# Attention transposes of the mixing stage move from the middle of a gate projection to the seam between two projections, one unit later

## The chip, the cores and the metric

The kernel runs on one core of one Trainium2 chip. The metric is the device time of one execution in microseconds (us), as the median of several runs. The engines are TensorE (PE for its matmuls, PEld for its weight loads), VectorE (DVE), ScalarE (ACT), GpSimd (POOL) and SyncE (SP), which starts the transfers. They run side by side and wait for each other on semaphores. Matmuls write to PSUM, which has eight banks of 512 fp32 columns for each partition.

## The reference, cut to what matters

A transformer block (feed-forward, token mixing, feed-forward) is followed by two layers of another kind. 256 tokens of width 2048 go through all of them. The change touches the token mixing alone:

```python
proj = h @ w_in                       # queries, keys, values of three mixers; then 3 x 2048 gate columns
o_a = _dilated_mixer(...)             # 12 heads in three groups, 4 outputs
o_b = _sink_swa_mixer(...)            # 8 heads, banded, with sinks
o_c = _nsa_mixer(...)                 # 12 heads; compressed, selected and windowed keys
gates = sigmoid(br_gate)
merged = gates[0] * (o_a @ w_branch_a) + gates[1] * (o_b @ w_branch_b) + gates[2] * (o_c @ w_branch_c)
return merged @ w_out
```

Each mixer computes softmax(q k + bias) v for each head.

## The kernel before

**Weights.** Every weight matrix comes as a numbered sequence of slabs (128 x 1024 fp32). SP loads a slab into a ring of four staging buffers. ACT rounds it to its high part (L1538, counted by `hi_done`). POOL (L852) or DVE (L2041) computes the low part, which is the difference. Here the split slabs lie in a ring of three. PE multiplies both parts: 16 matmuls with the high part (L900) and 8 with the low part (L906). A matmul and its weight load make a pair. Four slabs of 24 matmuls make one *product*, which is 256 output columns of a projection for all 256 tokens. It accumulates in one PSUM bank. Banks 0 and 2 alternate from product to product.

**Gates and attention side by side.** The gate columns are 24 products, steps 0 to 23. The attention is cut into 24 *units*: units 0 to 3 for the first mixer (kind a), 4 to 11 for the second (kind b), 12 to 23 for the third (kind c). A unit is a pair of heads and one half of the tokens: T=1 (the later half, which sees two blocks of keys) for even units and T=0 for odd ones. On PE a unit has three parts:

- *scores* (`scores_of`, L1246): q times k into banks 4 to 6. The contraction has 64 rows, so the trace names their tile 64\*128.
- *transposes* (`transposes_of`, recorded at L890 in its helper): the probabilities, block by block, into banks 1, 7 and 5. Their tile is 128\*128, as that of a product. There are 12 or 6 for kind a, 4 or 2 for kind b, 10 or 6 for kind c.
- *V products* (`values_of`, L1265): into 64 rows of bank 3, tile 128\*64. Kind c has four more with 15 rows of contraction. PE records two matmuls for each score and for each V product.

Between them DVE adds the bias and takes the maximum (`bias_of`), ACT takes the exponential (`exps`, L1729), DVE divides (`normalise`), and ACT copies the transposed blocks from PSUM to SBUF (`pt_copies`, L1740 and L1743). After the V products DVE copies the output out (`head_out`, L2323). Probabilities and their transposed copies have two buffers, one for each T.

**The order is written out by hand** for each engine. PE at step s runs the scores of unit s, two slabs of product s, the transposes of unit s-1, the other two slabs, and the V products of unit s-1. ACT copies the blocks of unit s-1 at the end of its step s, and DVE runs `head_out` of unit s-2 in step s. After step 23 come the branch matmuls. For them the output of every fourth unit is rounded and split (`heads_hi`, `heads_rest`). The transposes of unit 23 follow the first slab of the first branch, its V products the second slab. In `transposes_of` PE waits for the probabilities and for the copies of the unit before; in `values_of` for the unit's copies and the output copy of the unit before; in `scores_of` for the bias of the unit before.

Of the kernel before, what the change touches and what calls it, by code (L numbers as in the profile page):

```python
# [25 lines left out]
P = 128  # L26
S = 256
# [14 lines left out]
NCMP, CMP_STRIDE, CMP_END = 15, 16, 31  # L42
# [69 lines left out]
VALUES = {7: (0, 2), 8: (2, 2), 9: (4, 2), 12: (6, 1), 16: (7, 1), 17: (8, 1)}  # L112
CMP_GROUP = 0
LAST_OF = ((0, 6, 9), (4, 12, 12), (12, 17, 17))
HEADS_AT = {6: 0, 10: 1, 14: 2, 18: 3, 22: 4}
A_COLS, B_Q, C_Q, C_KV = 2304, 2304, 3072, 3840
CGATE0, GATE0 = 4608, 4644
# [7 lines left out]
SL_A, SL_B, SL_C = slopes(12), slopes(8), slopes(12)  # L125
# [158 lines left out]
def build(nc, a, out, const, marks, final):  # L284

    ctx = ExitStack()
    with ctx:
# [353 lines left out]
        def units_mix():  # L641
# [31 lines left out]
            for j in range(6):  # L673
                for T in (1, 0):
                    n = (T + 1) * P
                    w = 2 * n + NCMP
                    q, cd = qk[:, 17 + j, :], cst("cdist")[:, T * NCMP:(T + 1) * NCMP]
                    big = {(g, i): segment(4 + 2 * g, i * n, g * w + i * n, n, q, qk[:, 23 + i, :], g, T, dist_of(4, T), SL_C[j + 6 * g])
                           for g in range(2) for i in range(2)}
                    small = [segment(5 if T else 4 + 2 * g, g * S if T else 2 * n, g * w + 2 * n, NCMP, q, kc[:, :], g, T, cd, SL_C[j + 6 * g])  # L680
                             for g in range(2)]
                    segs = [small[0], big[1, 0], big[0, 0], big[1, 1], big[0, 1], small[1]]
                    blks = [block_of(g, g * w + i * n + kb * P, P, vn[:, kb, 7 + i, g * DH:(g + 1) * DH])
                            for i in range(2) for kb in range(T + 1) for g in range(2)]
                    blks += [block_of(g, g * w + 2 * n, NCMP, vc[0:NCMP, g, :]) for g in range(2)]
                    unit(T, w, segs, blks, 6 + j, kind="c", gate=j,
                         softmax=[(g * w + at, m) for g in range(2) for at, m in ((2 * n, NCMP), (0, n), (n, n))])
# [197 lines left out]
        def _(pe):  # L885
# [432 lines left out]
            def product_midway(step):  # L1318

                if step > 0:  # L1320
                    if step == 1:
                        pe.wait_ge(*act_out.after("gn"))
                    transposes_of(first[step - 1])
                else:
                    pe.wait_ge(*act_out.after("pln", PROJ - 1))
                    scores_of(first[0])

            for step in range(len(first)):
                for unit, normed, values in LAST_OF:
                    if step == unit:  # L1330
                        pe.wait_ge(*vec_out.after("qk", normed))
                        pe.wait_ge(*act_out.after("vn", values))
                if step == 12:
                    pe.wait_ge(*vec_out.after("kc"))
                if step > 0:
                    scores_of(first[step])
                product(gg + 1 + step, sA + 4 * step, midway=step)
                if step == 0:
                    pe.wait_ge(evacuated, gg + 1)
                    pe.wait_ge(*act_out.after("vn", PROJ - 1))  # L1340
                    for T in range(TT):
                        last = transpose(ps[:, 7, T * 36:T * 36 + 36], u(CTMP, 36, S)[:, T * P:(T + 1) * P])
                    last.then_inc(*pe_out.mark("gn"))
                else:
                    values_of(first[step - 1])


            def heads(c):
# [4 lines left out]
            for _k in range(4):  # L1353
                for half in range(2):
                    pe.wait_ge(evacuated, g - 1)
                    last = split_passes(acc(g), n, heads(0), True, True, chunks=2, width=512, col0=half * W2)
                    last.then_inc(*((slab_done, 1) if half == 1 else part_done.mark(g)))
                    g += 1
                n += 1
                if _k == 0:  # L1360
                    transposes_of(first[-1])
                if _k == 1:
                    values_of(first[-1])
# [153 lines left out]
        def _(act):  # L1517
# [234 lines left out]
            for step in range(len(first) + 1):  # L1752
                n = sA + 4 * step
                round_upto(n + 2)
                if step == 1:
                    act.wait_ge(*pe_out.after("gn"))
                    for T in range(TT):
                        last = fn(gn[:, T, :], ps[:, 7, 36 * T:36 * T + 36], ACT.Tanh, scale=half_rstd[:, T:T + 1])
                    last.then_inc(*act_out.mark("gn"))
                if step > 0:  # L1760
                    p = step - 1
                    act.wait_ge(evacuated, gg + 1 + p + 1)
                    fn(merged[:, 2 * p:2 * p + 2, :], merged[:, 2 * p:2 * p + 2, :], ACT.Tanh, scale=0.5).then_inc(*act_out.mark("gate", p))
                if step < len(first):
                    round_upto(n + (3 if step else 5))
                    exps(first[step])
                    round_upto(n + 4)
                if step > 0:
                    pt_copies(first[step - 1])
                if step in HEADS_AT:  # L1770
                    heads_hi(HEADS_AT[step], step - 3)
            n = sA + 4 * GATES
            round_upto(n + 6)
            heads_hi(5, -1)
            n += 12
# [121 lines left out]
        def _(dve):  # L1897
# [435 lines left out]
            for step in range(len(first) + 1):  # L2333
                if step > 0:
                    p = step - 1
                    dve.wait_ge(slab_done, sA + 4 * step)
                    v.tensor_tensor(merged[:, 2 * p:2 * p + 2, :], acc(gg + 1 + p).rearrange("p (c s) -> p c s", c=2), by_token(2), ALU.mult
                                    ).then_inc(evacuated, 1)
                if step < len(first):
                    slab_lo(sA + 4 * step + 2)  # L2340
                    bias_of(first[step])
                if step > 1:
                    head_out(first[step - 2])
                if step - 1 in HEADS_AT:
                    heads_rest(HEADS_AT[step - 1])
                if step == 2:
                    dve.wait_ge(*act_out.after("gn"))
                    chained(v.tensor_scalar(gn[:, :, :], gn[:, :, :], 0.5, 0.5, ALU.mult, ALU.add), "gn")
                if step < len(first):
                    normalise(first[step])  # L2350
# [18 lines left out]
            for pair in range(8):  # L2369
                dve.wait_ge(*((slab_done, n + pair // 2 + 1) if pair % 2 else part_done.after(g)))  # L2370
                merge(0, pair, g)
                g += 1
                if pair == 5:
                    head_out(first[-1])
            n += 4
# [389 lines left out]
```

## Time and profile before

| | |
|---|---|
| median of 3 runs | 3058.35 us (3056.56 to 3059.95) |
| the profiled execution | 3059.76 us |
| its span, first to last instruction | 3057.9 us |
| mean granted clock of TensorE | 0.999 |
| PE matmuls | 18842, busy 3038.1 us (99% of the span) |
| DVE, ACT, POOL busy | 66%, 48%, 43% |
| the 24 steps of gates and attention | about 970 to 1299 us of the span |

The profiled execution is 1.4 us above the median of the runs. The table is read from the span and the busy shares: how often an engine works says only whether it can be the bound. Where PE is busy without a gap, its time is the time from the start of one group of matmuls to the start of the next. A row of the timeline gives the start of a group and the time to the end of its last matmul. Matmuls overlap, and their ends are modelled, so what a group costs PE is the difference of two starts.

### The profile page before, as it was taken

The numbers are of one execution on the slowest core, as the hardware profiler recorded it, in microseconds if no ns is written. First come the engines' busy times: TensorE is split into PE (matmuls) and PEld (weight loads), VectorE is DVE, ScalarE is ACT, GpSimd is POOL, SyncE is SP. The second block draws the span as 40 slices with busy tenths as digits, with TensorE's granted clock in tenths as the row PEclk, the third lists the DMA queues.
The fourth block names the chain that finished last, engine by engine and source line by source line (L and its number), as shares of the span: only waits on it lengthen the run. The fifth ranks groups of instructions, "written<-read, shape, count | busy, mean of one in ns | idle before, by whom it ended". The sixth has DMA issues, their size and how long they took to land.

```text
span 3057.9 us, 46756 instructions
## 1 busy us (share of the span) xinstructions
PE 3038.1 (99%) x18842; PEld 2691.0 (88%) x18842; DVE 2009.3 (66%) x2972; ACT 1462.8 (48%) x1922; POOL 1305.8 (43%) x646
## 2 busy tenths in 40 slices
PE   8999999999999999999999999999999999999998
PEld 7888888888999999998888888888999998999987
DVE  4777666664324446787566666577579867689764
ACT  5444444444667445544544444444544454534454
POOL 5455545445556555595544455444340004610013
PEclk9999999999999999999999999999999999999999
DMA  6877787885776554465688887787576445655455
GB/s 218 287 269 260 273 282 246 289 285 183 225 170 177 157 161 145 150 174 200 216 272 279 269 271 263 261 287 268 180 207 191 156 141 197 182 185 177 155 163 179
DMA packets 486896, 661.17 MB, mean 216 GB/s; under 512 B 70024, under 2 KB 273528, under 8 KB 486424
## 3 DMA queue, kind: packets, MB, share of 16 engines
q1 hardware_dynamic: 481192, 653.74, 65.9%
q0 software_dynamic: 4448, 2.94, 0.3%
q8 instruction: 148, 2.42, 0.3%
q10 hardware_dynamic: 1040, 1.52, 0.1%
q14 instruction: 68, 0.56, 0.1%
HBM read 653.89 MB, written 2.10 MB: 215 GB/s over the span
## 4 chain that ended last, share of the span: by engine, by line
PE 96%; DVE 2%; ACT 1%; DMA 0%; issue 0%; POOL 0%; DVEq 0%; ACTq 0%
PE ps L1014 36%; PE ps L900 23%; PE ps L1019 18%; PE ps L906 11%; PE ps L890 1%; PE ps L1474 1%; PE ps L1265 1%; PE ps L1246 1%; PE ps L953 1%; DVE narrow_split_slabs L2041 0%; PE ps L985 0%; PE ps L1096 0%; PE ps L958 0%; PE ps L1303 0%; PE ps L1273 0%
## 5 line engine op out<-in xcount | busy, mean ns | idle before, releaser
L852 POOL TENSOR_TENSOR split_slabs<-stage,split_slabs 128x1024 fp32r<-128x1024 f32 x318 | 777.8, 2447 | 1315.1 <-ACT split_slabs L1538 1315.1
L1538 ACT ACTIVATE split_slabs<-stage 128x1024 fp32r<-128x1024 f32 x592 | 626.8, 1060 | 870.1 <-PE ps L1019 816.7
L1014 PE MATMUL ps<-split_slabs,h_split 128*128 128x512 f32 x3296 | 817.7, 390 | 1.0 <-ACT split_slabs L1538 0.9
L1538 ACT ACTIVATE narrow_split_slabs<-stage 128x1024 fp32r<-128x1024 f32 (+1 forms) x437 | 457.0, 1051 | 628.2 <-PE ps L906 537.8
L1014 PEld LDWEIGHTS ps<-split_slabs,h_split 128*128 128x128 f32 x3296 | 619.6, 188 | 130.7 <-issue 1.3
L900 PE MATMUL ps<-h_split,narrow_split_slabs 128*128 128x256 f32 x5696 | 726.9, 281 | 0.3 <-ACT narrow_split_slabs L1538 0.3
L900 PEld LDWEIGHTS ps<-h_split,narrow_split_slabs 128*128 128x128 f32 x5696 | 684.7, 189 | 13.5 <-issue 8.3
L2041 DVE TENSOR_TENSOR split_slabs<-stage,split_slabs 128x1024 fp32r<-128x1024 f32 x274 | 358.4, 1309 | 462.3 <-ACT split_slabs L1538 460.8
L852 POOL TENSOR_TENSOR narrow_split_slabs<-stage,narrow_split_slabs 128x1024 fp32r<-128x1024 f32 (+1 forms) x184 | 446.0, 2433 | 348.8 <-ACT narrow_split_slabs L1538 348.7
L1019 PE MATMUL ps<-split_slabs,h_split 128*128 128x512 f32 x1648 | 441.4, 390 | 0.8 <-DVE split_slabs L2041 0.5
L2041 DVE TENSOR_TENSOR narrow_split_slabs<-stage,narrow_split_slabs 128x1024 fp32r<-128x1024 f32 x253 | 330.6, 1309 | 138.2 <-ACT narrow_split_slabs L1538 137.5
L906 PE MATMUL ps<-h_split,narrow_split_slabs 128*128 128x256 f32 x2848 | 387.2, 279 | 0.8 <-POOL narrow_split_slabs L852 0.6
L1019 PEld LDWEIGHTS ps<-split_slabs,h_split 128*128 128x128 f32 x1648 | 309.6, 188 | 66.5 <-DVE split_slabs L2041 1.3
L906 PEld LDWEIGHTS ps<-h_split,narrow_split_slabs 128*128 128x128 f32 x2848 | 354.9, 189 | 1.4 <-POOL narrow_split_slabs L852 1.0
L1014 PE MATMUL ps<-split_slabs,act_split 128*128 128x512 f32 x1392 | 344.2, 390 | 0.0
L1014 PEld LDWEIGHTS ps<-split_slabs,act_split 128*128 128x128 f32 x1392 | 261.4, 188 | 54.5
L1019 PE MATMUL ps<-split_slabs,act_split 128*128 128x512 f32 x696 | 186.1, 389 | 0.0
L2103 DVE STREAM_TRANSPOSE ps<-U 32x256 f32<-32x256 f32 x352 | 160.3, 455 | 5.0
L1019 PEld LDWEIGHTS ps<-split_slabs,act_split 128*128 128x128 f32 x696 | 130.7, 188 | 27.2
L2057 DVE SCALAR_TENSOR_TENSOR ps<-U,cact,ps 128x512 f32<-128x512 f32 x192 | 145.1, 756 | 6.8
L2054 DVE SCALAR_TENSOR_TENSOR ps<-U,cact,ps 128x512 f32<-128x512 f32 x168 | 126.1, 751 | 21.1 <-DMA U<-in_w_ada 19.0
L2467 DVE SCALAR_TENSOR_TENSOR U<-U,params 128x256 f32<-128x256 f32 x240 | 110.7, 503 | 0.0
(302 smaller groups left out, 2272.9 us busy)
## 6 DMA issues: line engine op xcount, KB each, us to landing
stage<-in_w_in SPq DMA_DIRECT2D x357, 512.0 KB, 3.5
stage<-in_ffn_w_gu SPq DMA_DIRECT2D x352, 512.0 KB, 4.8
U<-in_w_ada SPq DMA_DIRECT2D x192, 512.0 KB, 5.5
stage<-in_ffn_w_down SPq DMA_DIRECT2D x176, 512.0 KB, 5.2
stage<-in_w_out SPq DMA_DIRECT2D x96, 512.0 KB, 4.1
stage<-in_w_in SPq DMA_DIRECT2D x80, 128.0 KB, 2.8
stage<-in_w_branch_c SPq DMA_DIRECT2D x32, 192.0 KB, 3.4
stage<-in_cmp_w SPq DMA_DIRECT2D x8, 512.0 KB, 5.3
```

The costliest lines, as they stand in the source:

```text
L852: nc.gpsimd.tensor_tensor(slab_part(n, 1, size(n)), stage[:, n % RING, 0:size(n)], slab_part(n, 0, size(n)).bitcast(F32), ALU.subtract).th ...
L890: return nc.tensor.transpose(dst, src, ident[0:n, 0:n])
L900: mm(bank[:, c * S:(c + 1) * S], w[0][:, kk, at:at + P], moving(kk, i), start=first and c == 0 and kk == 0 and i == 0, stop=False)
L906: ins = mm(bank[:, c * S:(c + 1) * S], w[1][:, kk, at:at + P], moving(kk, 0), start=False, stop=last and c == outs - 1 and kk == chunks - 1)
L1014: mm(ps[:, 2 * pair + T, :], stationary(kk, i)[:, T * P:(T + 1) * P], w[0][:, kk, :], start=first and kk == 0 and i == 0, stop=False)
L1019: ins = mm(ps[:, 2 * pair + T, :], stationary(kk, 0)[:, T * P:(T + 1) * P], w[1][:, kk, :], start=False, stop=last and kk == WK - 1)
L1538: return fn(slab_part(n, 0, size(n)), stage[:, n % RING, 0:size(n)], ACT.Copy)
L2041: v.tensor_tensor(slab_part(n, 1), stage[:, n % RING, :], slab_part(n, 0).bitcast(F32), ALU.subtract).then_inc(lo_vec, 1)
L2054: ins = v.scalar_tensor_tensor(total, w[:, 0, :], cact[:, 2 * k:2 * k + 1], total, ALU.mult, ALU.add)
L2057: v.scalar_tensor_tensor(total, w[:, 1, :], cact[:, 2 * k + 1:2 * k + 2], total, ALU.mult, ALU.add).then_inc(ada_load, 1)
L2103: last = v.transpose(dst[turned_rows, :, :, rows], src[rows, :, :, turned_rows])
L2467: ins = v.scalar_tensor_tensor(cy[:, c, :], src, col, cy[:, c, :], ALU.mult, ALU.add)
```

## The change

From unit 4 on (`SHALLOW = 4`), the transposes no longer interrupt a product. Before product s, PE runs the V products of unit s-3, the transposes of unit s-2 and the scores of unit s, one behind the other (`between_steps`). So transposes come half a product later than they did and V products almost one product later; the order of units stays. Units 0 to 3 keep their place, since their 12 blocks fill all of bank 5. For kind c and T=1, the two small scores move to columns 256 and 384 of bank 5, so that the transposed blocks in columns 0 to 255 can lie beside them. ACT's copies and DVE's output copies are taken one step later. The last units run on into the first branch: the V products of unit 22 behind its first slab, ahead of the transposes of unit 23. No operation is added or removed.

```diff
+SHALLOW = 4
-                    small = [segment(5 if T else 4 + 2 * g, g * S if T else 2 * n, ...
+                    small = [segment(5 if T else 4 + 2 * g, S + g * P if T else 2 * n, ...
...
                 if step > 0:
                     if step == 1:
                         pe.wait_ge(*act_out.after("gn"))
-                    transposes_of(first[step - 1])
+                    if step - 1 < SHALLOW:
+                        transposes_of(first[step - 1])
...
+            def between_steps(step):
+
+                if step - 3 >= SHALLOW:
+                    values_of(first[step - 3])
+                if step - 2 >= SHALLOW:
+                    transposes_of(first[step - 2])
+                if 0 < step < len(first):
+                    scores_of(first[step])
...
-                if step > 0:
-                    scores_of(first[step])
+                between_steps(step)
                 product(gg + 1 + step, sA + 4 * step, midway=step)
...
-                else:
+                elif step - 1 < SHALLOW:
                     values_of(first[step - 1])
+            between_steps(len(first))
...
                 if _k == 0:
+                    values_of(first[-2])
                     transposes_of(first[-1])
                 if _k == 1:
                     values_of(first[-1])
...
-                if step > 0:
+                if 0 < step <= SHALLOW:
                     pt_copies(first[step - 1])
+                if step - 2 >= SHALLOW:
+                    pt_copies(first[step - 2])
...
             n = sA + 4 * GATES
+            pt_copies(first[-1])
             round_upto(n + 6)
...
-                if step > 1:
+                if 1 < step < SHALLOW + 2:
                     head_out(first[step - 2])
+                if step - 3 >= SHALLOW:
+                    head_out(first[step - 3])
...
+                if pair == 1:
+                    head_out(first[-2])
                 if pair == 5:
                     head_out(first[-1])
```

## Rows read from the trace of the kernel before

**Rows 1.** Page, part 1: busy time, share of the span, instructions.

```profile
PE 3038.1 (99%) x18842; PEld 2691.0 (88%) x18842; DVE 2009.3 (66%) x2972; ACT 1462.8 (48%) x1922; POOL 1305.8 (43%) x646
```

**Rows 2.** Page, part 4: the chain that ended last, by engine.

```profile
PE 96%; DVE 2%; ACT 1%; DMA 0%; issue 0%; POOL 0%; DVEq 0%; ACTq 0%
```

**Rows 3.** Windows: length, busy of PE, PEld, DVE, ACT, POOL; clock, DMA share, GB/s.

```profile
1024.00:1310.00 286.00, 286.00 (x2574) 273.32 (x2573) 165.81 (x356) 151.52 (x325) 152.05 (x64) 1.00 0.51 153
```

**Rows 4.** Timeline of PE, steps 6 to 8: start, us to last end.

```profile
1056.37 1.98 PE L900 MATMUL ps<-h_split,narrow_split_slabs 128*128 128x256 f32 x16
...
1059.09 0.38 PE L890 MATMUL ps<-base_consts,U 128*128 128x128 f32 x2
1059.23 2.13 PE L900 MATMUL ps<-h_split,narrow_split_slabs 128*128 128x256 f32 x16
1061.20 1.10 PE L906 MATMUL ps<-h_split,narrow_split_slabs 128*128 128x256 f32 x8
1062.14 2.05 PE L900 MATMUL ps<-h_split,narrow_split_slabs 128*128 128x256 f32 x16
1064.02 1.11 PE L906 MATMUL ps<-h_split,narrow_split_slabs 128*128 128x256 f32 x8
1065.06 0.44 PE L1265 MATMUL ps<-U 128*64 128x128 f32 x4
1065.43 0.49 PE L1246 MATMUL ps<-U 64*128 64x128 f32 x4
...
1071.41 0.60 PE L890 MATMUL ps<-base_consts,U 128*128 128x128 f32 x4
1071.77 2.13 PE L900 MATMUL ps<-h_split,narrow_split_slabs 128*128 128x256 f32 x16
...
1077.60 0.66 PE L1265 MATMUL ps<-U 128*64 128x128 f32 x8
1078.19 0.70 PE L1246 MATMUL ps<-U 64*128 64x256 f32 x4
```

**Rows 5.** Timeline of PE, products of steps 14 and 16 (kind c, T=1).

```profile
1160.83 2.05 PE L900 MATMUL ps<-h_split,narrow_split_slabs 128*128 128x256 f32 x16
...
1163.65 0.82 PE L890 MATMUL ps<-base_consts,U 128*128 128x128 f32 x6
...
1186.73 2.15 PE L900 MATMUL ps<-h_split,narrow_split_slabs 128*128 128x256 f32 x16
```

**Rows 6.** Timeline of PE, first later layer: L1273 its scores, L1295 its V products.

```profile
2373.79 0.60 PE L890 MATMUL ps<-base_consts,U 128*128 128x128 f32 x4
2374.32 1.14 PE L1273 MATMUL ps<-U 64*128 64x256 f32 x8
...
2387.14 1.09 PE L1295 MATMUL ps<-U 128*64 128x128 f32 x16
2388.17 0.66 PE L890 MATMUL ps<-base_consts,U 128*128 128x128 f32 x4
2388.58 0.36 PE L900 MATMUL ps<-h_split,narrow_split_slabs 128*128 128x256 f32 x1
```

**Rows 7.** Groups, 2212 to 2297 us (first layer): busy, mean ns of one.

```profile
L900 PE MATMUL ps<-h_split,narrow_split_slabs 128*128 128x256 f32 x499 | 61.8, 276 | 0.0
```

**Rows 8.** Groups, 2655 to 2733 us (second layer), the same line.

```profile
L900 PE MATMUL ps<-h_split,narrow_split_slabs 128*128 128x256 f32 x448 | 57.3, 281 | 0.0
```

**Rows 9.** Groups, 1302 to 1368 us (branches), L900.

```profile
L900 PE MATMUL ps<-heads_split,narrow_split_slabs 128*128 128x256 f32 x376 | 48.1, 277 | 0.0
```

**Rows 10.** Timeline of ACT, step 16: rounding behind the exponentials, copies of transposed blocks.

```profile
1193.43 1.05 ACT L1538 ACTIVATE narrow_split_slabs<-stage 128x1024 fp32r<-128x1024 f32 x1
1194.38 0.58 ACT L1740 ACTIVATE U<-ps 128x512 f32<-128x512 f32 x1
1194.86 0.36 ACT L1743 ACTIVATE U<-ps 15x256 f32<-15x256 f32 x1
```

More of the change, by code:

```diff
@@ L679, in units_mix @@
                            for g in range(2) for i in range(2)}
-                    small = [segment(5 if T else 4 + 2 * g, g * S if T else 2 * n, g * w + 2 * n, NCMP, q, kc[:, :], g, T, cd, SL_C[j + 6 * g])
+                    small = [segment(5 if T else 4 + 2 * g, S + g * P if T else 2 * n, g * w + 2 * n, NCMP, q, kc[:, :], g, T, cd, SL_C[j + 6 * g])
                              for g in range(2)]
```

## The prediction

> **What bounds the kernel now.** I read the busy shares first: PE is busy for 3038.1 of 3057.9 us [rows 1]. The chain of work that ended last says the same in another way, since 96% of it is PE [rows 2]. An engine that is merely busy could still stand in this stage for a wait, so I took a window over steps 4 to 23 and the start of the branches: PE is busy for 286.00 of 286.00 us, at the full granted clock [rows 3]. The three engines around it work for 53 to 58% of that window. So no wait of PE exists here that a later place of the transposes could take away. What the change can move is only how much PE time the same matmuls take, and that is read from differences of starts in PE's timeline.
>
> Three things show there. The first is the pace of a product. One slab of 24 matmuls takes 1059.09 - 1056.37 = 2.72 us in the first half of step 6 [rows 4], but 1163.65 - 1160.83 = 2.82 us in the first half of step 14 [rows 5]. The clock is the same. The pace changes only where other work stands between two slabs, and is kept until the next such place. In each of the 19 products of steps 5 to 23 exactly one half is slow: the first in the even steps from 14 on, the second in all others. The two starts give 0.10 us a slab; the later layers, where the same instruction takes 276 or 281 ns [rows 7, 8], give 24 x 5 ns = 0.12. I take 0.105, so a slow half of two slabs costs 0.21 us. The second is the price of each seam. The third is that ACT and DVE have their work for a unit done long before PE asks for it.
>
> **The change part by part.** Nothing is computed more or less, no transfer or slab is touched, and the queues of SP and POOL keep their order. The sum therefore has a term for seams, one for pace, and one for new waits.
>
> *Seams removed.* After transposes in the middle of a product, the first 16 matmuls take 1061.20 - 1059.23 = 1.97 us, against 1064.02 - 1062.14 = 1.88 for the next 16 in the same pace [rows 4]. So going back from transposes to a product costs 0.09 us. It is paid 20 times before (units 4 to 23) and twice after (units 22 and 23, which still stand ahead of branch matmuls): -18 x 0.09 = -1.6 us. Going from a product into transposes costs nothing that I can see. Going from a product into V products costs about 0.1 (1065.06 - 1064.02 = 1.04 for 8 matmuls against 1062.14 - 1061.20 = 0.94), but that happens 20 times in both kernels: units 4 to 21 in seams, 22 and 23 in the branch.
>
> *Seams added.* Transposes now stand directly ahead of scores, 18 times (steps 6 to 23). This stage has no such pair, but the later layers do: four transposes ahead of scores take 2374.32 - 2373.79 = 0.53 us [rows 6], four ahead of a product 1071.77 - 1071.41 = 0.36 [rows 4]. The difference is 0.17, and 18 x 0.17 = +3.1 us. V products stand directly ahead of transposes 19 times (units 4 to 22). In the later layer the V products take 2388.17 - 2387.14 = 1.03 us for 16, and the four transposes behind them 2388.58 - 2388.17 = 0.41 instead of 0.36 [rows 6]. In this stage 4 V matmuls take 0.37 and 8 take 0.59 [rows 4], which is 0.055 each and 0.15 more at the end; by that 16 take 1.03, so the end is the same whatever follows. I take 0.05 a time: 19 x 0.05 = +1.0 us. From scores into a product nothing changes.
>
> The seams come to -1.6 + 3.1 + 1.0 = +2.5 us. The bounds for this term: if neither new seam costs anything (they could hide in the pause behind the V products), -1.6; if each costs what the dearest seam here costs, 0.17, then -1.6 + 37 x 0.17 = +4.7. I stay at +2.5, since the later layers run the same two pairs.
>
> A rule speaks to this. The Trainium skill, "TensorEngine Tiling (Array Packing)", section Key Properties, says that changing the tiling mode, and not just the tile, drains TensorE. By it a step before has three changes (product to V products, to scores, to product), with the transposes free since they share the product's tile; a step after has four. By the rule alone nothing would be saved in the middle of the product and the seams would come to +4.1; the trace has 0.09 us there that the rule does not explain, so the rows' +2.5 stands.
>
> *Pace.* A product without interruption has one pace for all four slabs. Which one, the seam ahead of it decides, and no row shows the new seam. If all 19 products are fast, the 19 slow halves go: 19 x -0.21 = -4.0 us. If all are slow, 19 fast halves turn slow: +4.0. Between these ends I go by what stands last before the product, which stays the scores. Before, the product behind the scores starts in the fast pace for kind b and for T=0 of kind c, and in the slow one behind the scores of T=1 of kind c in the 5 even steps from 14 on [rows 4, 5]. If that is kept, 5 x 2 = 10 halves are slow instead of 19: -9 x 0.21 = -1.9 us. This choice is the weakest of the text. The later layers show that whole products can run through in either pace [rows 7, 8].
>
> *Waits.* V products of unit s-3 need its copies by ACT, now made in step s-1. In step 16, the kind with the longest exponentials, these are over when the rounding starts at 1193.43, and the copies end at 1194.86 + 0.36 = 1195.2 [rows 10]. The product of that step starts at 1186.73 [rows 5], so they end 8.5 us into it, and some 9 us with one copy of 0.5 us more, as the ten blocks need that such a step copies after the change; an uninterrupted product lasts 4 x 2.72 = 10.9 us and more. The slack is 2 us, and the cover is the product itself. If ACT were later than that, PE would stand still with transposes, scores and the next product queued behind it, and DVE's bias would be late next. The transposes' probabilities are a whole product old, and the bias on DVE waits for transposes that run just ahead of its own scores. I cost all waits at 0. ACT's copies in the old place waited for PE's transposes once per step; now they are ready at once, which gives slack to the next rounding but nothing to PE, as PE never waited for it. At the end, the V products and transposes of units 21 to 23 are the same work in another order between the same slabs: 0.
>
> The sum is +2.5 - 1.9 = +0.6 us. The profiled execution (span 3057.9 and 1.9 around it) would go from 3059.76 to 3060.4, and the median, which is 1.4 us lower, from 3058.35 to 3059.0 us.
>
> **The rivals.**
>
> *All merged products in the slow pace.* +2.5 + 4 = +6.5 us, 3064.9. For it: slow pace follows transposes in nearly every step here, and transposes are now in every seam. Against it: the scores still stand last in the seam, and behind them 14 of 19 products start fast. It ends slower than before by 0.21%; it decides when at least 18 of 19 products are slow. Chance 0.10.
>
> *All fast, seams as costed.* +2.5 - 4 = -1.5 us, 3056.9. For it: the layer stage keeps the fast pace for whole products behind other work [rows 7]. Chance 0.20; within 0.2%.
>
> *All fast and the new seams free.* -1.6 - 4 = -5.6 us, 3052.7. Against it are rows 6, which show both pairs at a price. Chance 0.04. With anything that I don't see on top it would pass 0.2%.
>
> *A new wait of PE on ACT's copies*, where the exponentials slip by more than the 2 us of slack in the five or six steps of kind c with T=1. Each us beyond it costs 6 us in all, so it decides from 1 us on: 3059 + 6 = 3065. Nothing in the trace slips by so much. Chance 0.04.
>
> *The pace carries on.* The branch matmuls, from 1302 to 1368 us, run at 277 ns, fast [rows 9]. If the new seam ahead of them left them slow they would take 0.105 more on 2.72, 4% of 66 us or +2.5 us, and 3061.5. Chance 0.12.
>
> **How the numbers follow.** The forecast has the remaining 0.50. About 0.2% (6.1 us) is what a measurement of this kernel can tell from no change. Forecast, fast case and carried pace lie within it. The slow rival lies at its edge and the wait beyond it, together 0.14, of which I count 0.09 as slower by over 0.2%. Of faster I count 0.05. The rest, 0.86, is no change. The range has to hold 8 in 10: from 3055.5, just below the fast case, to 3063.0, which takes in the carried pace and leaves out the two slower rivals and the free seams.
>
> **What would show it right or wrong.** In the changed kernel's timeline of PE, a product of steps 5 to 23 should be one run of four slabs, each 2.72 us or each 2.82; their starts give the pace term. Transposes ahead of scores should cost 0.17 us more than ahead of a product, those behind V products 0.05 more. PE should stay busy without a gap in the stage, and ACT's copies should end before the V products. The prediction is wrong if PE shows idle time ahead of L1265 or L890, if the stage is over 6 us shorter or longer, or if the time moves outside this stage.

## The result

The changed kernel takes 3063.34 us in the median of 19 runs (3060.83 to 3064.91), the kernel before 3057.98 us in 19 runs beside them (3055.41 to 3059.95). The ratio is 1.0018, with a 95% interval of 1.0011 to 1.0024: about 5.4 us slower, where 0.6 us was forecast. The change is small, but it is real. The profiled executions are 3064.40 and 3059.76 us, their spans 3062.6 and 3057.9 us.

The busy shares of the kernel after, the first part of its page, answer to [rows 1]:

```profile
PE 3041.9 (99%) x18842; PEld 2691.6 (88%) x18842; DVE 2018.0 (66%) x2972; ACT 1466.1 (48%) x1922; POOL 1308.3 (43%) x646
```

The same instructions, with PE busy 3.8 us longer; the span has grown by 4.7 us, so nearly 1 us is a new idle time. The window that read 286.00 of 286.00 before [rows 3] now shows it (length, busy of PE, PEld, DVE, ACT, POOL, clock, DMA share, GB/s):

```profile
1024.00:1310.00 286.00, 284.69 (x2530) 268.82 (x2530) 177.72 (x354) 150.44 (x324) 147.65 (x62) 1.00 0.54 152
```

PE is idle for 1.31 us, and DVE is busy for 12 us longer with two operations fewer. Both have one cause, below: it is DVE's divisions that take longer (62.5 us of this window before, 77.0 after). The clock is at its full level in both.

The seam and the products in PE's timeline of the kernel after: the seam ahead of step 8 (V products of unit 5, transposes of unit 6, scores of unit 8), and the product behind it; then steps 12 and 13.

```profile
1076.36 0.44 PE L1266 MATMUL ps<-U 128*64 128x128 f32 x4
1076.73 0.66 PE L891 MATMUL ps<-base_consts,U 128*128 128x128 f32 x4
1077.32 0.70 PE L1247 MATMUL ps<-U 64*128 64x256 f32 x4
1077.95 2.15 PE L901 MATMUL ps<-h_split,narrow_split_slabs 128*128 128x256 f32 x16
...
1080.88 2.05 PE L901 MATMUL ps<-h_split,narrow_split_slabs 128*128 128x256 f32 x16
...
1083.71 2.05 PE L901 MATMUL ps<-h_split,narrow_split_slabs 128*128 128x256 f32 x16
...
1089.46 0.66 PE L1266 MATMUL ps<-U 128*64 128x128 f32 x8
...
1130.55 2.10 PE L901 MATMUL ps<-h_split,narrow_split_slabs 128*128 128x256 f32 x16
...
1133.39 1.98 PE L901 MATMUL ps<-h_split,narrow_split_slabs 128*128 128x256 f32 x16
...
1136.11 1.98 PE L901 MATMUL ps<-h_split,narrow_split_slabs 128*128 128x256 f32 x16
```

Two things are to be seen. Four transposes take 1077.32 - 1076.73 = 0.59 us where they took 0.36 ahead of a product [rows 4]. And a merged product has one pace throughout: 2.83 us a slab at step 8 (1083.71 - 1080.88), 2.72 at step 12 (1136.11 - 1133.39). Such a product lasts 11.50 us in the slow pace and 11.09 in the fast one. Steps 6 to 11, 13, 16, 18, 20 and 22 are slow, 11 of 19.

The idle time is in the first branch matmuls. The timeline of the kernel after, all engines, with the idle time and its releaser in brackets:

```profile
1294.74 1.05 ACT L1550 ACTIVATE narrow_split_slabs<-stage 128x1024 fp32r<-128x1024 f32 x1
...
1295.88 4.75 POOL L853 TENSOR_TENSOR narrow_split_slabs<-stage,narrow_split_slabs 128x1024 fp32r<-128x1024 f32 x2 [0.68 <-ACT narrow_split_slabs L1550]
...
1295.92 2.38 DVE L2331 TENSOR_TENSOR rden<-rden,gn 128x6 f32<-128x6 f32 x1
...
1297.09 1.06 ACT L1550 ACTIVATE narrow_split_slabs<-stage 128x1024 fp32r<-128x1024 f32 x1 [0.56 <-PE ps L907]
...
1298.34 5.41 DVE L2333 TENSOR_SCALAR U<-U,rden 128x15 f32<-128x15 f32 x6
...
1299.64 0.66 PE L1266 MATMUL ps<-U 128*64 128x128 f32 x8
...
1300.94 2.39 POOL L853 TENSOR_TENSOR narrow_split_slabs<-stage,narrow_split_slabs 128x1024 fp32r<-128x1024 f32 x1 [0.32 <-ACT narrow_split_slabs L1550]
...
1301.66 1.19 PE L901 MATMUL ps<-heads_split,narrow_split_slabs 128*128 128x256 f32 x8
...
1303.67 0.68 DVE L2352 TENSOR_TENSOR U<-ps,rstd_b 128x512 f32<-128x512 f32 x1
...
1304.40 1.20 PE L901 MATMUL ps<-heads_split,narrow_split_slabs 128*128 128x256 f32 x8 [1.08 <-DVE U L2352]
...
1305.87 0.36 ACT L1755 ACTIVATE U<-ps 15x256 f32<-15x256 f32 x1
...
1306.28 1.09 PE L1266 MATMUL ps<-U 128*64 128x128 f32 x16 [0.23 <-ACT U L1755]
```

Product 23 ended at 1299.6, just ahead of the V products at 1299.64. DVE could take it out of PSUM only at 1303.67, since six divisions of unit 23 (L2333) stood ahead of it and took 5.41 us. The row names the first of them, with 15 columns; the fourth has 15 columns too, the other four have 128. The second half-slab of branch A needs that bank, and PE stood for 1.08 us, and for 0.23 us more ahead of the V products of unit 22. Those waited for ACT's copies, which had stood behind an ACT operation that needs the same evacuation. From the first branch matmul to these V products PE takes 1306.28 - 1301.66 = 4.62 us. Without the stall it takes 3.01, as the experiment with the evacuation first shows; the stall costs 1.6 us. The kernel before, in DVE's timeline of the same place:

```profile
1294.35 2.37 DVE L2316 TENSOR_TENSOR rden<-rden,gn 128x6 f32<-128x6 f32 x1
1296.75 1.15 DVE L2318 TENSOR_SCALAR U<-U,rden 128x15 f32<-128x15 f32 x6
1299.50 0.69 DVE L2337 TENSOR_TENSOR U<-ps,rstd_b 128x512 f32<-128x512 f32 x1 [1.60 <-PE ps L906]
```

There the same six take 1.15 us, and the evacuation starts at 1299.50. The difference lies with POOL, whose timeline before was:

```profile
1294.30 2.39 POOL L852 TENSOR_TENSOR narrow_split_slabs<-stage,narrow_split_slabs 128x1024 fp32r<-128x1024 f32 x1 [0.69 <-ACT narrow_split_slabs L1538]
1297.87 2.39 POOL L852 TENSOR_TENSOR narrow_split_slabs<-stage,narrow_split_slabs 128x1024 fp32r<-128x1024 f32 x1 [1.18 <-ACT narrow_split_slabs L1538]
```

The 15-column division that DVE begins while POOL computes a low part ends with POOL's operation. Before, POOL had a gap of 1.18 us, from 1296.69 to 1297.87, and the six divisions, from 1296.75 to 1297.90, just fitted into it. After, POOL's operations stand back to back. The first division lasts 2.32 us, until the second of the pair is over at 1300.63. The fourth begins just behind the start of POOL's next operation and lasts 2.39 us, until that is over at 1303.33. The four of 128 columns take 0.28 us each. The gap went because ACT's roundings now come closer together, 2.35 us apart (1294.74, 1297.09), since no transposes hold up PE's product in the middle and the slabs' buffers come free sooner.

**The balance.** From the start of step 5 (1040.55 before, 1039.80 after) to the last instruction the kernel after loses 0.75 + 4.7 = 5.4 us. The products of steps 5 to 23 take 215.2 us instead of 216.4, so -1.2. The transposes take 4.2 us more. The stretch from the end of step 23 to the last V products takes 1.8 us more, unit for unit, of which the stall is 1.6. The branch matmuls behind those V products, to the first matmul of the output projection, take 1373.67 - 1312.16 = 61.5 us instead of 1368.66 - 1308.07 = 60.6, so +0.9. The last 0.3 us, with the other sign, lies behind them. There the work is the same in every kernel of this document, and its time varies by 1.5 us between their profiles, so I read nothing into it.

The 0.9 us is the pace again. In the branches of the kernel before a slab of 18 matmuls takes 1337.61 - 1335.57 = 2.04 us, in the kernel after 1341.87 - 1339.75 = 2.12:

```profile
1335.57 1.52 PE L900 MATMUL ps<-heads_split,narrow_split_slabs 128*128 128x256 f32 x12
...
1337.61 1.52 PE L900 MATMUL ps<-heads_split,narrow_split_slabs 128*128 128x256 f32 x12
```

```profile
1339.75 1.58 PE L901 MATMUL ps<-heads_split,narrow_split_slabs 128*128 128x256 f32 x12
...
1341.87 1.58 PE L901 MATMUL ps<-heads_split,narrow_split_slabs 128*128 128x256 f32 x12
```

The branches after are fast up to the slab of 1336.86. Its second matmul comes 0.07 us late, and from there on all are slow. In the kernel before the same slab has a like delay, 0.08 us, and the pace stays fast.

### The profile page after: what moved, and what is told of

Its sections match the earlier page's. It is cut to its first block, busy times and chain, and to the rows that moved or that the text cites. A ratio compares the mean times of both kernels' runs of the same rounds, so it can differ in the third digit from the quotient of the medians.

```text
span 3062.6 us, 46755 instructions
## 1 busy us (share of the span) xinstructions
PE 3041.9 (99%) x18842; PEld 2691.6 (88%) x18842; DVE 2018.0 (66%) x2972; ACT 1466.1 (48%) x1922; POOL 1308.3 (43%) x646
## 4 chain that ended last, share of the span: by engine, by line
PE 96%; DVE 2%; ACT 1%; issue 0%; POOL 0%; DMA 0%; ACTq 0%; DVEq 0%
PE ps L1015 36%; PE ps L901 23%; PE ps L1020 18%; PE ps L907 11%; PE ps L891 2%; PE ps L1486 1%; PE ps L1266 1%; PE ps L1247 1%; PE ps L954 1%; DVE narrow_split_slabs L2056 0%; PE ps L986 0%; PE ps L1097 0%; PE ps L959 0%; PE ps L1304 0%; PE ps L1274 0%
```

## The experiments

Ratios are to the kernel before, run beside each. Those with a single run are read from the profile. The time ahead of step 5, whose work is the same in all of them, varies by 4 us between the profiles, so two profiles are best compared from the start of step 5; the kernel before takes 2017.4 us from there to the end.

| experiment | median us (runs) | ratio, interval | span | from step 5 | slow products of 19 | stall in the branch |
|---|---|---|---|---|---|---|
| kernel after | 3063.34 (19) | 1.0018, 1.0011 to 1.0024 | 3062.6 | 2022.8 | 11 | yes |
| transposes first | 3055.56 (10) | 0.9994, 0.9985 to 1.0004 | 3052.8 | 2015.1 | 1 | yes |
| transposes last | 3056.37 (10) | 0.9997, 0.9987 to 1.0007 | 3055.8 | 2016.4 | 6 | yes |
| only the last units | 3060.81 (10) | 1.0011, 1.0002 to 1.0021 | 3060.8 | 2019.9 | only one is merged, fast | yes, longer |
| evacuation first | 3060.49 (10) | 1.0010, 1.0001 to 1.0019 | 3058.7 | 2020.7 | 11 | no |
| transposes and evacuation first | 3053.96 (11) | 0.9989, 0.9980 to 0.9998 | 3051.4 | 2014.0 | 1 | no |
| short low parts | 3060.99 (1) | | 3059.2 | 2020.1 | 11 | no |
| one more wait | 3062.18 (10) | 1.0014, 1.0005 to 1.0023 | 3060.4 | 2022.0 | 11 | yes |
| one more instruction | 3065.19 (1) | | 3063.3 | 2022.0 | 11 | yes |
| one more transpose | 3062.81 (1) | | 3060.9 | 2020.1 | 0 | yes |
| two more transposes | 3063.08 (1) | | 3061.2 | 2022.9 | 3 | yes |

### Transposes first in the seam

```diff
             def between_steps(step):
-                if step - 3 >= SHALLOW:
-                    values_of(first[step - 3])
                 if step - 2 >= SHALLOW:
                     transposes_of(first[step - 2])
+                if step - 3 >= SHALLOW:
+                    values_of(first[step - 3])
```

> The changed kernel, with the three groups of a seam in the order transposes, V products, scores. Theory: what costs in the changed kernel is a group whose tile differs from the one ahead of it; transposes share the product's tile, so this order has three changes of tile per step as the kernel before has, not four. The 18 pairs of transposes ahead of scores (0.17 us more each) and the 19 pairs of V products ahead of transposes (0.05 more each) go: four transposes ahead of V products take about 0.45 us instead of 0.59, the V products' entry stays at about 0.1, so the run is about 4 us below the changed kernel, near 3059.5 us, plus or minus 2 us by the pace of the products. The wait in the first branch stays. Rival, the seams cost for being crowded and not for their order: within 1 us of the changed kernel's 3063.3. Rival, the time is in the later copies and evacuations: no difference either.

PE's timeline, the seam ahead of step 9 (transposes of unit 7, V products of unit 6, scores of unit 9):

```profile
1086.12 0.38 PE L891 MATMUL ps<-base_consts,U 128*128 128x128 f32 x2
1086.43 0.66 PE L1266 MATMUL ps<-U 128*64 128x128 f32 x8
1087.02 0.49 PE L1247 MATMUL ps<-U 64*128 64x128 f32 x4
1087.44 2.11 PE L901 MATMUL ps<-h_split,narrow_split_slabs 128*128 128x256 f32 x16
...
1090.29 1.98 PE L901 MATMUL ps<-h_split,narrow_split_slabs 128*128 128x256 f32 x16
```

The median is 7.8 us under that of the kernel after, which has the same work and the same lateness of units, and lower than was expected, since the pace changed as well. From the start of step 5 the profiles differ by 7.7 us. The two transposes take 0.31 us instead of 0.37, so the price behind V products is gone. The product takes 11.00 us where the fast one after takes 11.09. That is its end and not its start: the first slab behind the scores takes 1090.29 - 1087.44 = 2.85 us here and 1133.39 - 1130.55 = 2.84 in the kernel after, but this product ends in transposes, which it enters for nothing, and not in V products, which cost 0.1. These two give 18 x (0.06 + 0.09) = 2.7 us. Ten products fewer are slow, 10 x 0.41 = 4.1 us. The branch matmuls stay fast, 60.6 us instead of 61.5. Together that is the 7.7. Moving transposes into the seam is therefore not what costs; the order within the seam is.

### Transposes last in the seam

```diff
-                if step - 2 >= SHALLOW:
-                    transposes_of(first[step - 2])
                 if 0 < step < len(first):
                     scores_of(first[step])
+                if step - 2 >= SHALLOW:
+                    transposes_of(first[step - 2])
```

> The changed kernel, with the order V products, scores, transposes, so the transposes stand directly ahead of the product. Theory of the tiles: three changes per step as well, but the step from transposes to a product costs 0.09 us as it did in the kernel before: 18 x 0.09 = 1.6 us above the order with the transposes first, some 2.5 us below the changed kernel, near 3061, and the bias of DVE starts about a microsecond later, which is hidden. Rival on the pace: what stands last ahead of the product decides its pace; in the kernel before a product was slow behind transposes in 19 of 25 cases, so most of the 19 products would be slow, +2 to +3 us, and the kernel would be near 3063 to 3064 again.

```profile
1087.94 0.49 PE L1247 MATMUL ps<-U 64*128 64x128 f32 x4
1088.37 0.44 PE L891 MATMUL ps<-base_consts,U 128*128 128x128 f32 x2
1088.56 2.07 PE L901 MATMUL ps<-h_split,narrow_split_slabs 128*128 128x256 f32 x16
```

These rows of PE's timeline are the seam ahead of step 9, behind its V products. The median is below both expectations, 3061 and 3063 to 3064. Two transposes take 0.19 us ahead of a product and 0.37 ahead of scores (1090.41 - 1090.04 in the kernel after): the 0.17 of the prediction, taken away. Six products are slow: 13, 16, 18, 20 and 22, as in the kernel after, and 14, which is fast there. Steps 6 to 11 are fast. Together with the first experiment this shows the prices of the neighbours directly, and that the pace comes and goes with the order of the seam.

### Only the last units

```diff
-SHALLOW = 4
+SHALLOW = 22
```

> The changed kernel with SHALLOW = 22: only the last two units are taken late, everything else is as before. Theory: 1.56 us of the loss is a wait behind the last gate product: without the transposes in its middle, ACT's roundings come 2.4 us apart instead of 3.6, POOL computes two low parts without a gap, DVE's multiplications of unit 23 take 5.4 us instead of 1.2, the evacuation of product 23 comes 4 us late, and PE stands still ahead of the second half-slab of the first branch. This needs only the last step: about +1.5 us over the kernel before, near 3059.5, with the same PE gap of about 1.1 us in the first branch. Rival, the wait grows out of the whole deferred chain: no gap here and 3058.

Here steps 5 to 22 are those of the kernel before, start for start (each 0.41 us later), and only units 22 and 23 are late. PE and DVE in their timelines:

```profile
1303.23 1.20 PE L901 MATMUL ps<-heads_split,narrow_split_slabs 128*128 128x256 f32 x8 [2.15 <-DVE U L2352]
```

```profile
1297.17 5.41 DVE L2333 TENSOR_SCALAR U<-U,rden 128x15 f32<-128x15 f32 x6
1302.50 0.68 DVE L2352 TENSOR_TENSOR U<-ps,rstd_b 128x512 f32<-128x512 f32 x1
```

The stall is there alone, and larger than expected (2.15 us of idle time), since no V products stand between product 23 and the branch here, while DVE takes the product out as late as in the kernel after (4.1 us behind its end, against 4.0). The kernel is 3.3 us slower than before in the median, and 2.5 us in the profiles from the start of step 5, without one new seam in steps 5 to 21. One product without a pause is enough to close POOL's gap.

### The evacuation of product 23 ahead of the divisions

```diff
                 slab_lo(...), evacuation of the product before, head_out(...)
...
+                if step == len(first):
+                    normalise(first[-1])
...
-                if step < len(first):
+                if step < len(first) - 1:
```

On DVE, unit 23 is divided only behind the evacuation of product 23 and the output copy of unit 21.

> The changed kernel, with DVE evacuating the last gate product and copying out unit 21 ahead of the divisions of unit 23. Theory: the wait of PE in the first branch goes (1.26 us ahead of the second half-slab and 0.3 ahead of the V products of unit 22), so about 1.5 us below the changed kernel, near 3061.8; the divisions of unit 23 end in time for its transposes. Rival, the wait has another cause, such as the copies of unit 22 on ACT: no difference, 3063.3.

```profile
1297.90 0.69 DVE L2352 TENSOR_TENSOR U<-ps,rstd_b 128x512 f32<-128x512 f32 x1 [7.91 <-PE ps L907]
...
1299.50 2.02 DVE L2325 TENSOR_SCALAR den<-den 128x6 f32<-128x6 f32 x1
...
1301.99 1.15 DVE L2333 TENSOR_SCALAR U<-U,rden 128x15 f32<-128x15 f32 x6
```

PE in its timeline, the first branch matmul and the V products of unit 22:

```profile
1299.81 1.19 PE L901 MATMUL ps<-heads_split,narrow_split_slabs 128*128 128x256 f32 x8
...
1302.82 1.09 PE L1266 MATMUL ps<-U 128*64 128x128 f32 x16
```

In DVE's timeline the evacuation comes as soon as the product is done, and PE has no gap; the divisions are over at 1303.14, in time for the transposes of unit 23. The 11 slow products are the same ones. The median falls by 2.9 us against the kernel after, more than the stall's 1.6 us (1302.82 - 1299.81 = 3.01 instead of 4.62). The intervals of the two ratios overlap (their ratios differ by 0.0008, or 2.4 us), but the profiles show a second term: the branch matmuls behind stay fast, 60.6 us instead of 61.5. The row of L2325 is the collision once more, with another operation: 6 columns, begun while POOL's operation of 1299.10 ran, are over at 1301.52, and POOL's at 1301.50.

### Transposes first and evacuation first

Both edits together.

> The changed kernel with both mends: transposes first in every seam, and DVE evacuating the last gate product and copying out unit 21 ahead of the divisions of unit 23. If the two are separate terms, they add up: 1.5 us below the kernel with the transposes first alone, near 3054.0 us, and 3.5 us (0.11%) below the kernel before, with no idle time of PE in the first branch. Rival: the pace of the branch or of a later stage turns slow behind the new order and takes the 1.5 us back, 3055.5.

It came out at 3053.96 us, 1.6 us under the kernel with the transposes first alone, as expected, and 3.9 us under the kernel before (ratio 0.9989, interval 0.9980 to 0.9998) and 9.4 under the kernel after. This is the version that beats both. In its window from 1024 to 1310 us PE is busy for 286.00 us again:

```profile
1024.00:1310.00 286.00, 286.00 (x2597) 272.50 (x2594) 175.36 (x360) 152.64 (x327) 155.27 (x65) 1.00 0.56 156
```

That is 2597 matmuls in the same time that held 2574 before.

### Short low parts on POOL

```diff
+                w = P if n in (S_GATES + 4 * GATES, S_GATES + 4 * GATES + 1) else size(n)
-                nc.gpsimd.tensor_tensor(slab_part(n, 1, size(n)), ...
+                nc.gpsimd.tensor_tensor(slab_part(n, 1, w), ...
```

Of the first two slabs of the branches POOL computes the low part in 128 of 1024 columns only; the rest is left out. The order of every queue is that of the kernel after.

> The changed kernel, in which POOL computes the low part of the first two branch slabs on 128 of their 1024 columns only; this leaves most of the low product of these two slabs out. Theory: POOL's back-to-back low parts hold up DVE's divisions of unit 23, of which two with 15 columns take 2.3 us each instead of 0.24. With the short ones the six divisions take about 1.2 us in all and end near 3.5 us ahead of where they did, the last gate product is evacuated as it ends, and PE's wait of 1.26 us in the first branch is gone. Rival: DVE is held up by something else (its own queue, the exponentials on ACT): the divisions still take 5.4 us and the wait stays.

DVE and POOL in their timelines:

```profile
1295.68 1.15 DVE L2334 TENSOR_SCALAR U<-U,rden 128x15 f32<-128x15 f32 x6
1299.06 0.69 DVE L2353 TENSOR_TENSOR U<-ps,rstd_b 128x512 f32<-128x512 f32 x1 [2.22 <-PE ps L908]
```

```profile
1295.17 0.46 POOL L854 TENSOR_TENSOR narrow_split_slabs<-stage,narrow_split_slabs 128x128 fp32r<-128x128 f32 x1 [0.67 <-ACT narrow_split_slabs L1551]
1297.53 0.46 POOL L854 TENSOR_TENSOR narrow_split_slabs<-stage,narrow_split_slabs 128x128 fp32r<-128x128 f32 x1 [1.90 <-ACT narrow_split_slabs L1551]
```

With POOL out of the way the same divisions take 1.15 us, the evacuation starts as the product ends, and the stall is gone. DVE's code was not touched, so the lengthening of the divisions is POOL's work. Here too the branch matmuls behind take 60.6 us.

### One more wait, one more instruction

The slow pace could have been a matter of PE's instruction stream. The first kernel has one more wait on a semaphore long since reached, ahead of each merged product:

```diff
                 between_steps(step)
+                if step > SHALLOW:
+                    pe.wait_ge(slab_done, sA)
```

> The changed kernel with one more wait of PE ahead of each merged product (steps 5 to 23), on a semaphore that was passed long before, so it adds an instruction to PE's queue and no time of its own. It asks what sets the pace of a product. If the place of a product in the instruction stream (odd or even) does, the 11 slow and 8 fast products of steps 5 to 23 change sides in part, by 0.44 us each. If the seam's matmuls and their order do, the pattern stays as it is: slow in steps 6 to 11, 13, 16, 18, 20 and 22, and the time stays at 3063.3.

It went into an instruction that waits anyway, so no instruction was added. The second kernel has another such wait on `lo_pool` behind it, which does add one:

> The changed kernel with two more waits of PE, both passed long before, ahead of each merged product. The one extra wait of the run before fitted into a wait instruction that stood there already and added none; two make one more instruction in PE's queue for each of the 19 products. If a product's pace follows its place in the instruction stream (odd or even), the pattern of slow products (6 to 11, 13, 16, 18, 20, 22) changes; if it follows from the seam's matmuls, the pattern stays and the time is that of the changed kernel, 3063, within 1 us.

Both have exactly the slow products of the kernel after: 6 to 11, 13, 16, 18, 20 and 22. Neither a wait that costs no time nor the count of instructions sets the pace. The second kernel's 3065.19 us is over the 3063 that was expected; it is a single run, and from the start of step 5 its profile is 0.8 us shorter than that of the kernel after.

### One and two more transposes in the seam

```diff
+                for _ in range(1 if un["key"][1] >= SHALLOW else 0):
+                    b = un["blocks"][0]
+                    transpose(pt_bank(0)[0:b["n"], :], un["E"][:, b["col"]:b["col"] + b["n"]])
```

From unit 4 on the first block of each unit is transposed twice, in the second kernel three times (`range(2 if ...`). It is work more, of 0.11 us each.

> The changed kernel, in which each of units 4 to 23 transposes its first block twice. The extra transpose costs 0.11 us, 20 x 0.11 = 2.2 us. It makes the number of pairs of weight load and matmul in a seam odd, where it is even in all kernels so far. If the pace follows which of two places for weights a product's first load goes to, then products change sides by this odd count: the slow ones are others than 6 to 11, 13, 16, 18, 20, 22. If the pace hangs on fine timing, the pattern may change as well, so this run alone doesn't tell the two apart; the run with two extra transposes does.

> The same with the first block transposed three times, 20 x 0.22 = 4.4 us over the changed kernel plus or minus the pace term. The count in a seam is even again. If the odd or even count sets the pace, the pattern of slow products is that of the changed kernel (6 to 11, 13, 16, 18, 20, 22); if it is fine timing at the seam, the pattern may be any.

PE's timeline of the first of them, at the same seam as shown after the change (ahead of step 8):

```profile
1077.15 0.77 PE L891 MATMUL ps<-base_consts,U 128*128 128x128 f32 x5
1077.85 0.70 PE L1247 MATMUL ps<-U 64*128 64x256 f32 x4
...
1081.32 1.98 PE L901 MATMUL ps<-h_split,narrow_split_slabs 128*128 128x256 f32 x16
...
1084.04 1.98 PE L901 MATMUL ps<-h_split,narrow_split_slabs 128*128 128x256 f32 x16
```

The slab now takes 2.72 us (1084.04 - 1081.32), and that in all 19 products. From the start of step 5 to the first matmul behind product 23 this kernel, with 18 more transposes in it, needs 1298.11 - 1040.85 = 257.3 us; the kernel after 1299.64 - 1039.80 = 259.8. So 2 us of work more made the stretch 2.6 us shorter, as 11 x 0.41 = 4.5 less 18 x 0.11 = 2.0 says. With two more transposes three products are slow (steps 8, 10 and 14). The pace thus follows what the seam holds: in each of the kernels of this document, all merged products behind the same kinds and numbers of matmuls in the same order have the same pace. It isn't simply odd or even: with two more, the parity is that of the kernel after, and yet 9 of its 11 slow products are fast and one other is slow.

## Why the prediction was wrong

**The bound: right, except for one place.** PE sets the time and nothing but its own order in the stage mattered up to 1302 us. "DVE have their work for a unit done long before PE asks for it" was true of the units, not of the evacuation behind them.

**Seams: right.** For the pairs that the prediction costed at 0.17 and 0.05, the transposes take 0.59 instead of 0.36 us for four and 0.37 instead of 0.14 for two, 0.23 each and +4.2 us in all, where 3.1 + 1.0 was forecast. Products save about 0.1 a time by not being interrupted, against 0.09. "From scores into a product nothing changes" held as well (2.84 and 2.85 us for the first slab in two orders). What the text did not see is that the same move has a cheaper order. It had the 0.1 us from a product into V products as paid in both kernels; with the transposes first it is not paid at all. Net of the pace term (+0.6, below), the products saved 1.2 + 0.6 = 1.8, so the seams came to 4.2 - 1.8 = +2.4 us; the +2.5 stands. By the rule of the Trainium skill, "TensorEngine Tiling (Array Packing)", Key Properties, the order chosen changes the mode four times a step and both other orders three times. The trace agrees on which is dearer: one change less saves 0.15 us a seam with the transposes first and 0.17 + 0.02 with them last (the product 11.07 instead of 11.09). It has more than the rule, since a product with its transposes in the middle also has three changes and pays 0.1 more than an uninterrupted one.

**Pace: wrong, the step "between these ends I go by what stands last before the product".** It gave 10 slow halves and -1.9 us. There were 22, so with 19 before +0.6: 2.5 us off. Of the five products that it called slow (14, 16, 18, 20, 22) four were. The scores did stand last in both kernels, and yet product 14 turned fast, and behind scores that had a fast product before, those of steps 6 to 11 and 13 turned slow. The ends of -4.0 and +4.0 were right, and "this choice is the weakest of the text" too. The last two experiments show why no such choice could be argued: a single transpose more in each seam turns all 11 fast.

**Waits: wrong, the steps "I cost all waits at 0" and, for the last units, "the same work in another order between the same slabs: 0".** I looked at who waits for ACT's copies, and in the steps those were indeed in time. I didn't look at what an uninterrupted product does to the engines that feed it: ACT rounds earlier, POOL's low parts close up, and DVE's divisions, which live in POOL's gaps, push the evacuation back. That is 1.6 us. The fourth experiment takes it away on DVE, the sixth on POOL, and the third has it without the new seams. The text named idle time ahead of the V products or transposes as a sign against it, and there it was, 0.23 us. The warning stood in the kernel before. DVE's timeline of step 16 there has the six divisions of another unit over two POOL operations; the two of 15 columns take 2.35 us each:

```profile
1194.64 5.66 DVE L2318 TENSOR_SCALAR U<-U,rden 128x15 f32<-128x15 f32 x6
```

In the middle of the stage PE had no gap from it; at the first branch the second half-slab needs the bank that DVE empties.

**The pace of the branches: wrong, taken as unchanged.** The rival of +2.5 us had them slow throughout, carried from the last seam. Product 23 was fast, and the branches were slow only from the slab of 1336.86 on: 0.9 us. They are slow in the kernel after, with one more wait, with one more instruction and with two more transposes, and fast in the seven others and in the kernel before. All four have the stall, but so have four kernels whose branches stay fast (transposes first, transposes last, only the last units, one more transpose). The kernels with the same slow products but without the stall stay fast as well.

So -1.9 became +0.6, 0 became +1.6 for the stall, and 0 became +0.9 for the branches. These are 5.0 us, where the measured 5.4 differs from +0.6 by 4.8. The rest, -0.2, is the sum of small terms: 0.2 more around the stall, 0.1 less in the seams, and 0.3 less behind the branches, which is within what that stretch varies by.

**What stays open** is what on the chip makes a product slow. It isn't the clock (1.00 in both), a wait that costs no time, the count of instructions or the parity of pairs. I can say which seams give which pace only by running them. Open too is why a delay of 0.07 us left the branches slow in four kernels and not in the others.

## What to carry to other kernels

When a pause of the bounding engine is taken away, look at the engines that lived in that pause, and at the first place where a buffer is needed soon: there the same lateness that was free elsewhere becomes a stall. When order alone is changed and no engine waits, try other orders of the groups, as the three tried here differ by up to 8 us, and weigh a guess about pace by its ends, not by its middle. An operation of one shape that shows two durations in one trace (0.23 and 2.35 us for a division of 15 columns) has to be read against the other engines before it is called covered.

## What the runs showed of the hardware

Some of DVE's small operations that begin during a low part on POOL end with POOL, whatever their size: in the kernel after 15 columns take 2.32 and 2.39 us instead of 0.23, and 6 columns 2.38 instead of 0.17; in the fourth experiment another operation of 6 columns takes 2.02. Of the 96 divisions in the kernel before, 24 begin with more than 0.1 us of a POOL operation still to run. Each of them ends with it or up to 0.42 us behind it. Twelve of these have 15 columns and take 2.34 or 2.35 us, where the other twelve of that shape take 0.22 to 0.24. It isn't so for every operation: the 12 reciprocals of two columns that begin during one take 0.17 us, and DVE's evacuation of PSUM takes 0.69 us at 1299.50 before, beside a POOL operation of 1297.87 to 1300.26.

The Trainium skill, "SBUF — State Buffer", section SBUF: two separate sides, states an exclusive lock on a port pair that DVE and GpSimd share: a DVE operation in a mode with two ports, or with two inputs in SBUF, and a GpSimd operation keep each other out for the whole instruction. The lengthened operations agree with it, and so does the evacuation, which has one of its inputs in PSUM. That the divisions run in such a mode, and why the reciprocals escape, no run here shows.

Fp32 matmuls of 256 columns run at 2.72 or 2.83 us for 24 pairs at the same full clock. In the gate stage the pace changes only at a foreign group, is kept for a whole product, and is repeated to 0.01 us by every kernel with the same seam. In the branches of four kernels it changed without one, at a slab whose second matmul came 0.07 us late. A group's price depends on its neighbours: transposes cost 0.17 us more ahead of V products or scores than ahead of a product, and 0.06 more behind V products.
